# Second block's experts: the two smaller sorted groups share one row tile, 13 units become 11

## The chip, the cores and the metric

The kernel runs on one core of one Trainium2 chip. The metric is the device time of one execution in microseconds (us). The kernel before takes 1627.51 us, the median of 3 runs (1626.91 to 1627.9).

## The reference, cut to what matters

Two blocks run one after the other on 256 tokens of width 1024, in f32. The first is a transformer-like block with 16 experts; the change doesn't touch it. The second has two layers; each is a mixer (attention in three kinds), a norm, and a hierarchical mixture of experts, then a norm again:

```python
lg = jnp.einsum('td,dg->tg', t, rg_w) + rg_b              # 4 groups
g_hot = one_hot(argmax(lg, -1))
le = einsum('tge,tg->te', einsum('td,gde->tge', t, re_w) + re_b, g_hot)   # 8 experts of that group
top_v, top_i = lax.top_k(le, 2)
gate = g_hot * (p_top * gate_e)
for g in range(4):
    h = silu(einsum('td,edf->tef', t, w_gate[g])) * einsum('td,edf->tef', t, w_up[g])
    y = y + einsum('tef,efd->td', h * gate[:, g, :, None], w_down[g])
```

So each token goes to one of 4 groups and there to 2 of 8 experts. An expert has a gate and an up matrix of 1024 x 256 and a down matrix of 256 x 1024: 3 MB in f32. The kernel loads all 32 experts of a layer, 96 MB, whatever the tokens choose.

## The kernel before, in words

**Rows and units.** A layer's experts are done group by group (x = 0 to 3). For a group, its tokens are gathered by a one-hot matrix `PG` into a row tile of at most 128 rows (`group_gather`, two halves); then the rows of each expert are gathered from that tile by a one-hot matrix `PX2` (`expert_gather(u, part)`) into a tile `XS2`, with 64 or 32 columns for each expert. A unit is what one pass of the array takes: 2 experts of 64 rows, or 4 experts of 32 rows. Group 0 has four units of two, in fixed order. Groups 1 to 3 are sorted on the chip by how many tokens an expert has: the four fullest make two units of two, the other four one unit of four. That is 4 + 3 x 3 = 13 units (`UNITS`, line 59).

**One turn of the loop.** In `experts_pe` turn p does, on TensorE: `gate_up(p)` (L1528), the gathers that were put behind it (`slots`, `group_gather`, both L640, `expert_gather`, L1508), `group_sum(p-3)` (L1574), `down(p-2)` (L1557), `turned(p-1)` (L645). At the last unit of a group its one-hot matrix is turned; in the turns of `SHARES` the group's result is spread to the tokens (`group_share`, L1164, from 4 banks). VectorE and ScalarE walk through the same turns in `experts_dve` and `experts_act`. After the last turn come some matmuls that keep the clock up (`keep_on`, L665), the branch of `overflow_pe`, `last_sum()` and the norm.

**The order of the loads.** All weights come in 2 MB blocks through a ring of seven slots, issued by SyncE (`sync`) in the order in which TensorE asks for them: `weights()` appends the key to `order`. A block is issued when TensorE has read the block seven before it. I number a layer's 48 blocks from 0. A unit of two has 2 gate/up blocks and 1 down block; a unit of four has 4 and 2. The turn's order gives gate/up blocks of unit p and then down blocks of unit p-2. Group 0's blocks are single 2 MB transfers (L3195). Blocks of sorted groups (`ranked`, L3154) are put together from 2 transfers of 1 MB or 4 of 512 KB, one for each expert, whose number SyncE reads from SBUF (L3147, 8 numbers at the first block of each group) after VectorE's `by_count` wrote them (`IDS`, L2444).

**The fallback.** Tokens over a capacity (128 rows in a group's tile, 64 or 32 for an expert) set a flag in turn `FLAG_AT`; if it is set, `overflow_pe` and its partners compute the layer's rest again with all 32 experts.

Of the kernel before, what the change touches and what calls it, by code (L numbers as in the profile page):

```python
# [52 lines left out]
CAP = 128  # L53
# [5 lines left out]
UNITS = [(0, j) for j in range(4)] + [(x, j) for x in range(1, 4) for j in range(3)]  # L59
# [4 lines left out]
def four(n):  # L64
    return UNITS[n][0] > 0 and UNITS[n][1] == 2

# [19 lines left out]
def width(u):  # L86

    return 128 if u > 1 and u % 2 else 256


def gathers_behind(n):

    x, j = UNITS[n]
    if x == 0:
        return [(j // 2 + 1, j % 2)]
    if j == 0:
        return [(2 * x + 1, 0), (2 * x + 1, 1)]
    return [(2 * x + 2, 0), (2 * x + 2, 1)] if j == 2 and x < 3 else []

SHARES, FLAG_AT = (8, 11, 13), 10
# [293 lines left out]
def program(nc, ring_d, ranked_d, p1_d, p2_d, pf_d, xT_d, cT_d, pos_d, out_d):  # L396
    order, slot_read = [], []
    with contextlib.ExitStack() as ctx:
# [162 lines left out]
        CAPE, KEY, IDS = take(32), take(4, 8), take(24).bitcast(I32)  # L561
        RK, CMP, PERM, GXP = take(3, 8), take(3, 8, 8), take(3, 8, 8), take(2, 8, 8)
# [563 lines left out]
        def norm_pe(g, l, fresh, turn, full, keep_on):  # L1126

            def last_group(b):
                ps = fresh("ffn", l, 3, b)
                group_share(g, l, 3, b, ps).then_inc(*full("ffn", l, 3, b))  # L1130

            def turned_rows(b):
                ps = PS[:, b, :]
                before, banks.last[b], banks.of["rt", l, b] = banks.last[b], ("rt", l, b), b
                g.wait_ge(*at(*before))
                g.wait_ge(*at("ffn", l, 3, b))
# [30 lines left out]
        def mixers_pe(g, l, fresh, weights, arrived, finished, group, turn, column_sum, across, full, keep_on):  # L1167
# [291 lines left out]
            group(ps[:, 0:32], [(ONES, SEL2[:, ti, 4:36]) for ti in range(2)]).then_inc(*full("cnt", l))  # L1459

        def experts_pe(g, l, weights, arrived, finished, group, turn, full, keep_on):
# [21 lines left out]
            def slots(x):  # L1483

                ps = high("gx", l, x)
                g.wait_ge(*at("posg", l))
                g.wait_ge(*at("gates", l))
                g.wait_ge(*at("pg", l, x > 0))
                group(ps[:, 0:16], [(PG[:, ti, x, :], POSG[:, ti, x, :]) for ti in range(2)]).then_inc(*full("gx", l, x))
# [21 lines left out]
            def gate_up(n):  # L1511
# [3 lines left out]
                for part in range(parts_):  # L1515
# [9 lines left out]
                    for kk in range(nk * part, nk * part + nk):  # L1525
                        for s in range(128 // m):
                            c = (0 if four(n) else (j % 2) * 128) + s * m
                            ins = g.matmul(ps[m * s:m * s + m, :], XS2[u % 2][:, kk, c:c + m], wv[:, kk % nk, s, :], start=kk == 0, stop=kk == 7)  # L1528
# [54 lines left out]
            for p in range(NU + 2):  # L1583
                if p < NU:
                    x, j = UNITS[p]
                    gate_up(p)
                    if j == 0 and x < 3:
                        slots(x + 1)
                    if p == 2:
                        turned_norm()  # L1590
                    if j < 2 and x < 3:
                        group_gather(x + 1, j)
# [29 lines left out]
        def overflow_pe(g, l, group, turn):  # L1622
            g.wait_ge(*at("flag", l))
            with g.If(g.value_load(FLG[0:1, 0:1].bitcast(I32)) > 0):
# [4 lines left out]
                for e in range(32):  # L1629
# [13 lines left out]
                    for m in range(8):  # L1643
                        if m >= 3:
                            g.wait_ge(*at("xrm", l, e, m - 3))
                        group(PS[:, (0, 1, 7)[m % 3], 0:256], [(wd[:, f, m * 128:(m + 1) * 128], XHD[:, f, :]) for f in range(2)]) \
# [451 lines left out]
        def norm_dve(v, l, out, settle, full):  # L2098
# [7 lines left out]
            for b in range(4):  # L2106
                add_share(v, l, 3, b, out, full)
# [37 lines left out]
        def mixers_dve(v, l, out, settle, full, scale_rows, affine, square):  # L2145
# [177 lines left out]
            v.memset(MR, -LOWEST).then_inc(*out())  # L2323
            for b in range(4):
# [85 lines left out]
            v.scalar_tensor_tensor(out=KEY, in0=bank("cnt", l)[:, 0:32].rearrange("p (g e) -> p g e", g=4), scalar=8.0,  # L2410
                                   in1=bc(p1("iotn", 1, 12)[:, :, 0:8], [128, 4, 8]), op0=ALU.mult, op1=ALU.add).then_inc(*out("cnt", l))

        def experts_dve(v, l, out, settle, full):
            sig.stage = f"e{l}"

            def slots(x):
                full("gx", l, x)
                if x == 0:
                    v.tensor_copy(GX[:, x, :], bank("gx", l, x)[:, 0:16]).then_inc(*out("gx", l, x))
                    return  # L2420
                settle()
                v.tensor_tensor(GXP, bc(bank("gx", l, x)[:, 0:16].rearrange("p (a o e) -> p a o e", a=2, o=1), [128, 2, 8, 8]),
                                bc(PERM[:, x - 1:x, :, :], [128, 2, 8, 8]), ALU.mult).then_inc(*out("gx", l, x))
                settle()
                v.tensor_reduce(out=GX[:, x, :], in_=GXP.rearrange("p a r e -> p (a r) e"), op=ALU.add, axis=AX.X, negate=False).then_inc(*out())

            def by_count():

                for x in range(3):
                    v.tensor_tensor(CMP[:, x, :, :], bc(KEY[:, x + 1:x + 2, :], [128, 8, 8]),  # L2430
                                    bc(KEY[:, x + 1, :].rearrange("p (e o) -> p e o", o=1), [128, 8, 8]), ALU.is_ge).then_inc(*out())
# [3 lines left out]
                for x in range(3):  # L2435
                    v.tensor_tensor(PERM[:, x, :, :], bc(RK[:, x:x + 1, :], [128, 8, 8]),
                                    bc(p1("iota")[:, 0:8].rearrange("p (r o) -> p r o", o=1), [128, 8, 8]), ALU.is_equal).then_inc(*out())
                settle()
                for x in range(3):
                    v.tensor_tensor(CMP[:, x, :, :], PERM[:, x, :, :], bc(p1("iotn", 1, 12)[:, :, 0:8], [128, 8, 8]), ALU.mult).then_inc(*out())  # L2440
                settle()
                v.tensor_reduce(out=KEY[:, 1:4, :], in_=CMP, op=ALU.add, axis=AX.X, negate=False).then_inc(*out())
                settle()
                v.tensor_scalar(IDS, KEY[:, 1:4, :].rearrange("p g r -> p (g r)"), -1.0, 8.0, ALU.mult, ALU.add).then_inc(*out("ids", l))  # L2444

            def capacities():

                v.memset(CAPE[:, 0:8], CAPX + 0.5).then_inc(*out())
                v.tensor_scalar(CAPE[:, 8:32], RK.rearrange("p g e -> p (g e)"), 4.5, float(CAPX - CAPQ), ALU.is_lt, ALU.mult).then_inc(*out())
# [3 lines left out]

            def other_groups():
                for ti in range(2):
                    ins = v.tensor_tensor(PG[:, ti, 1:4, :], bc(PSX[:, ti, 1:4].rearrange("p (g o) -> p g o", o=1), [128, 3, 128]),
                                          bc(p1("iota", 1, 128), [128, 3, 128]), ALU.is_equal)
                ins.then_inc(*out("pg", l, 1))
# [17 lines left out]

            def places(x):
                if x >= 2:
                    full("xs2", l, 2 * (x - 2) + 1, 1, 1)
                    full("hd", l, last_unit(x - 2))  # L2480
                settle()
                cols = ((0, 8, 64),) if x == 0 else ((0, 4, 64), (4, 8, 32))
                for e0, e1, m in cols:
                    n, c0 = e1 - e0, 64 * e0
                    px, pxg = [X2[x % 2].rearrange("p e c -> p (e c)")[:, c0:c0 + n * m].rearrange("p (e c) -> p e c", c=m) for X2 in (PX2, PXG)]
                    ins = v.tensor_tensor(px, bc(GX[:, x, e0:e1].rearrange("p (e o) -> p e o", o=1), [128, n, m]),
                                          bc(p1("iota", 1, 128)[:, :, 0:m], [128, n, m]), ALU.is_equal)
                    ins.then_inc(*(out("px", l, x) if e1 == 8 else out()))
                settle()
                for e0, e1, m in cols:  # L2490
                    n, c0 = e1 - e0, 64 * e0
                    px, pxg = [X2[x % 2].rearrange("p e c -> p (e c)")[:, c0:c0 + n * m].rearrange("p (e c) -> p e c", c=m) for X2 in (PX2, PXG)]
                    ins = v.tensor_tensor(pxg, px, bc(GX[:, x, 8 + e0:8 + e1].rearrange("p (e o) -> p e o", o=1), [128, n, m]), ALU.mult)
                    ins.then_inc(*(out("pxg", l, x) if e1 == 8 else out()))
# [30 lines left out]
            places(0)  # L2525
            group_gather(0, 1)
            other_groups()
            expert_gather(0, 0)
            expert_gather(0, 1)
            by_count()  # L2530
            for p in range(NU + 2):
                if p < NU:
                    x, j = UNITS[p]
                    gate_up(p)
                    if j == 0 and x < 3:
# [5 lines left out]
                    if j < 2 and x < 3:  # L2541
                        group_gather(x + 1, j)
                        if j == 1:
                            places(x + 1)
# [11 lines left out]
                if p == FLAG_AT:  # L2556
                    capacities()
                    for ti in range(2):
                        v.tensor_tensor(GOV[:, ti, :, :], PSX[:, ti, 4:36].rearrange("p (g e) -> p g e", g=4),
                                        CAPE.rearrange("p (g e) -> p g e", g=4), ALU.is_gt).then_inc(*out())  # L2560
                        v.tensor_scalar(GOG[:, ti, :], PSX[:, ti, 0:4], float(CAP) + 0.5, None, ALU.is_gt).then_inc(*out())
# [5 lines left out]
                        .then_inc(*out("over", l))  # L2567
                    full("flag", l)
# [9 lines left out]
        def overflow_dve(v, l, settle):  # L2578
            v.wait_ge(*at("flag", l))
            with v.If(v.value_load(FLG[0:1, 0:1].bitcast(I32)) > 0):  # L2580
# [7 lines left out]
                for e in range(32):  # L2588
# [7 lines left out]
                    for m in range(8):  # L2596
                        v.wait_ge(*at("full", "xd", l, e, m))
                        v.tensor_tensor(R[:, m, :], R[:, m, :], PS[:, (0, 1, 7)[m % 3], 0:256], ALU.add).then_inc(*up("dve", "xrm", l, e, m))
# [429 lines left out]
        def experts_act(s, l, out, full):  # L3028
# [56 lines left out]
            for p in range(NU + 2):  # L3085
                if p < NU:
                    x, j = UNITS[p]
                    gate_up(p)
                    if j < 2 and x < 3:
                        group_gather(x + 1, j)  # L3090
# [36 lines left out]
        def sync(q):  # L3127
# [14 lines left out]

            def ranked(i, x, kind, l, group_, j, part):

                if (l, group_) not in experts:
                    q.wait_ge(*at("ids", l))
                    experts[l, group_] = [q.snap(q.value_load(IDS[0:1, 8 * (group_ - 1) + r:8 * (group_ - 1) + r + 1], min_val=0, max_val=7))  # L3147
                                          for r in range(8)]
                of = ranks(j)
                n = SLOT // len(of)  # L3150
                c = n * part + (4096 if kind == "dr" else 0)
                for s, r in enumerate(of):
                    src = ranked_d[3 * l + group_ - 1, bass.ds(experts[l, group_][r], 1), :, c:c + n].rearrange("o p c -> (o p) c")
                    q.dma_start(RING[x][:, s * n:(s + 1) * n], src).then_inc(*land(f"ring{x}", *(("landed", i) if s == len(of) - 1 else ())))  # L3154

            for i, (key, n) in enumerate(order):
# [39 lines left out]
                if key[0] == "dr" and key[2:] == (3, 2, 1):  # L3196
# [288 lines left out]
```

## Time and profile before

| | |
|---|---|
| median of 3 runs | 1627.51 us |
| the profiled execution's own time | 1627.17 us |
| its span, first to last instruction | 1625.4 us |
| TensorE busy in the span | 1407.9 us (87%) |
| 16 DMA queues, share of their time | 74% |
| bytes read from HBM | 490.21 MB |
| mean granted clock | 0.947 |

The execution takes 1.8 us more than its span. Busy shares are averages over stages: the first block's experts, then two times mixer, experts and norm. The second block's experts run from 923 to 1148 us (first layer) and from 1380 to 1603 us (second layer) of the span.

### The profile page before, as it was taken

To read this page: it belongs to the slowest core of one execution; us is meant where nothing else is said; L and a number is where in the kernel's file an instruction comes from. 1 tells how busy PE (TensorE), PEld (TensorE's weight loads), DVE (VectorE), ACT (ScalarE), POOL (GpSimd) and SP (SyncE) were. 2 spreads that over 40 slices of the span, in tenths; PEclk is the share of its full clock that TensorE was granted. 3 is DMA by queue.
4 is the path that set the end of the run, shared out by engine and by line. 5 is a ranking of instruction groups with operands and counts; after the bars stand their busy time and mean duration, and the time that the engine had idled before them with its cause. 6 is when DMAs were issued, how large, how long until landed. Compare 5 with 4: busy or idle time off the path is not lost. (4 is left out here: it accounts for less than half of the span.)

```text
span 1625.4 us, 19345 instructions
## 1 busy us (share of the span) xinstructions
PE 1407.9 (87%) x7684; PEld 789.8 (49%) x7684; DVE 509.0 (31%) x1140; ACT 314.1 (19%) x659; POOL 0.2 (0%) x4
## 2 busy tenths in 40 slices
PE   6999999856656566599999999997999989999978
PEld 4665877412311211166777644432667677444424
DVE  5225553101101101015763522221346744232213
ACT  2422202100000100112332312211223223122202
POOL 0000000000000000000000000000000000000000
PEclk9999999978877878899999999999999999999999
DMA  9465477999999999992321599999715214899993
GB/s 387 167 251 209 165 293 316 412 429 427 427 428 427 428 427 429 427 422 81 145 104 52 216 380 399 411 417 412 315 52 207 98 59 156 345 406 416 418 412 152
DMA packets 56386, 492.62 MB, mean 303 GB/s; under 512 B 6240, under 2 KB 6624, under 8 KB 25952
## 3 DMA queue, kind: packets, MB, share of 16 engines
q1 hardware_dynamic: 56144, 491.15, 74.0%
q8 instruction: 66, 1.08, 0.3%
q14 instruction: 32, 0.26, 0.0%
q10 hardware_dynamic: 144, 0.13, 0.0%
HBM read 490.21 MB, written 1.05 MB: 302 GB/s over the span
## 5 line engine op out<-in xcount | busy, mean ns | idle before, releaser
L640 PE MATMUL PS<-A 128*128 128x256 f32 (+6 forms) x1592 | 376.6, 393 | 5.3 <-ACT A L2624 1.5
L996 PE MATMUL PS<-A 128*32 128x512 f32 x1536 | 237.7, 757 | 135.0 <-DMA A<-ring_d 135.0
L640 PEld LDWEIGHTS PS<-A 128*128 128x128 f32 (+1 forms) x1592 | 277.9, 193 | 96.9 <-issue 57.3
L996 PEld LDWEIGHTS PS<-A 128*32 128x32 f32 x1536 | 52.7, 126 | 306.4 <-issue 238.5
L1528 PE MATMUL PS<-A 128*64 128x512 f32 (+1 forms) x1024 | 188.6, 608 | 12.5 <-DMA A<-ranked_d 12.2
L1528 PEld LDWEIGHTS PS<-A 128*64 128x64 f32 (+1 forms) x1024 | 57.1, 128 | 126.4 <-issue 124.6
L2058 DVE TENSOR_TENSOR A<-A,PS 128x512 f32<-128x512 f32 x8 | 5.5, 687 | 321.0 <-PE PS L996 321.0
L1557 PE MATMUL PS<-A 128*64 128x512 f32 (+1 forms) x512 | 94.9, 597 | 6.7 <-issue 4.7
L645 PE MATMUL PS<-A 128*128 128x128 f32 (+1 forms) x444 | 66.1, 279 | 17.8 <-DVE A L2058 7.1
L645 PEld LDWEIGHTS PS<-A 128*128 128x128 f32 (+1 forms) x444 | 50.0, 143 | 60.4 <-issue 36.0
L2509 DVE TENSOR_TENSOR A<-A,PS 128x256 f32<-128x256 f32 x26 | 11.0, 423 | 194.3 <-ACT A L3059 194.3
L1557 PEld LDWEIGHTS PS<-A 128*64 128x64 f32 (+1 forms) x512 | 27.4, 126 | 70.4 <-issue 66.1
L1391 PE MATMUL PS<-A 128*128 128x256 f32 x256 | 59.3, 383 | 2.3 <-DVE A L2323 1.2
L1391 PEld LDWEIGHTS PS<-A 128*128 128x128 f32 x256 | 47.5, 190 | 11.3 <-issue 3.9
L2515 DVE COPY A<-PS 128x512 f32<-128x512 f32 x26 | 18.0, 692 | 108.3 <-PE PS L1557 108.3
L1574 PE MATMUL PS<-A 128*128 128x512 f32 x104 | 49.5, 597 | 1.8 <-issue 1.8
L3059 ACT ACTIVATE A<-PS 128x256 f32<-128x256 f32 x26 | 10.0, 386 | 204.7 <-PE PS L1528 204.7
L1508 PE MATMUL PS<-A 128*128 128x256 f32 (+1 forms) x256 | 49.3, 343 | 0.0
L1508 PEld LDWEIGHTS PS<-A 128*128 128x128 f32 x256 | 41.0, 190 | 15.0 <-issue 11.4
L665 PE MATMUL PS<-A 128*128 128x256 f32 x156 | 37.5, 389 | 0.0
L2973 ACT ACTIVATE A<-A 128x128 f32<-128x128 f32 (+1 forms) x48 | 21.2, 443 | 73.4 <-DVE A L2285 73.4
L2504 DVE TENSOR_SCALAR A<-PS,A 128x256 f32<-128x256 f32 (+1 forms) x64 | 28.6, 489 | 18.3 <-PE PS L1508 17.6
(360 smaller groups left out, 1302.8 us busy)
## 6 DMA issues: line engine op xcount, KB each, us to landing
A<-ring_d SPq DMA_DIRECT2D x156, 2048.0 KB, 26.6
A<-ranked_d SPq DMA_DIRECT2D x72, 1024.0 KB, 14.2
A<-ranked_d SPq DMA_DIRECT2D x144, 512.0 KB, 15.1
A<-ring_d SPq DMA_DIRECT2D x2, 1312.0 KB, 22.1
A<-ring_d SPq DMA_DIRECT2D x2, 1280.0 KB, 25.2
A<-p_d SPq DMA_DIRECT2D x1, 1232.0 KB, 22.5
A<-xT_d SPq DMA_DIRECT2D x1, 1024.0 KB, 5.5
A<-cT_d SPq DMA_DIRECT2D x1, 1024.0 KB, 12.0
```

Of the source, the lines that this page charges most:

```text
L640: ins = g.matmul(out, l, r, start=n == 0, stop=n == len(pairs) - 1)
L645: return g.transpose(out, in_, ident[0:k, 0:k])
L665: ins = g.matmul(ps[:, 0:256], *(of or (ident, V(o1, 256))), start=True, stop=True)
L996: ins = g.matmul(ps[32 * e:32 * e + 32, :], rows_of(kk, e), wv[:, kk % 2, e, :], start=kk == 0, stop=kk == 7)
L1391: ins = g.matmul(bank("wo", l, b)[:, j * 256:(j + 1) * 256], w[:, k, c:c + 128], O[:, k, :], start=k == 0 and j == 0, stop=k == 7, skip_gr ...
L1508: ins = g.matmul(ps[:, c:c + w], XGT[:, x, d * 128:(d + 1) * 128], px, start=True, stop=True)
L1528: ins = g.matmul(ps[m * s:m * s + m, :], XS2[u % 2][:, kk, c:c + m], wv[:, kk % nk, s, :], start=kk == 0, stop=kk == 7)
L1557: ins = g.matmul(ps[m * s:m * s + m, :], HD[n % 2][:, f, m * s:m * s + m], wd[f][:, s, half * 512:(half + 1) * 512], start=f == 0, stop=f ...
L1574: ins = g.matmul(PS[:, b, :], QT[p % 2], YE2[p % 2][:, half * 512:(half + 1) * 512], start=n == 0, stop=last)
L2504: ins = v.tensor_scalar(XS2[u % 2][:, d, 0:w], bank("xs2", l, u, part, 1)[:, j * 256:j * 256 + w], gain, bias, ALU.mult, ALU.add)
L2515: v.tensor_copy(YE2[p % 2][:, 512:1024], bank("ye2", l, p, 1)).then_inc(*out("ye2", l, p, 1))
L2973: ins = s.activation(p, p, ACT.Exp, bias=ST[:, i, c:c + 1], scale=1.0, accum_out=ST[:, i, 4 + c:5 + c])
```

## The change

`UNITS` becomes 4 + 3 + 4 = 11 units. VectorE finds which of groups 1 to 3 holds the fullest expert (`largest_group`: a one-hot `BIG`). That group is x = 1, and is sorted as before. The other two are joined in one row tile x = 2 (`offsets`, `places_in_groups`): the second group's tokens stand behind the first's. Their 16 experts aren't sorted and are four units of four, 32 rows each. The capacity of 128 rows holds for the joined tile. SyncE reads four expert numbers after the block `("gu", 3, 0)`, four after `("gu", 3, 1)` and two group numbers after `("dn", 4)`, instead of eight at each group's first block. `group_gather` and `slots` of the next tile move to later turns, `FLAG_AT` from 10 to 9, the tests for it to turn 7.

```diff
-UNITS = [(0, j) for j in range(4)] + [(x, j) for x in range(1, 4) for j in range(3)]
+UNITS = [(0, j) for j in range(4)] + [(1, j) for j in range(3)] + [(2, j) for j in range(4)]
 def four(n):
-    return UNITS[n][0] > 0 and UNITS[n][1] == 2
+    return UNITS[n] == (1, 2) or UNITS[n][0] == 2
 def width(u):
-    return 128 if u > 1 and u % 2 else 256
+    return 128 if u == 3 else 256
 def gathers_behind(n):
     x, j = UNITS[n]
     if x == 0:
         return [(j // 2 + 1, j % 2)]
-    if j == 0:
-        return [(2 * x + 1, 0), (2 * x + 1, 1)]
-    return [(2 * x + 2, 0), (2 * x + 2, 1)] if j == 2 and x < 3 else []
-SHARES, FLAG_AT = (8, 11, 13), 10
+    if x == 2:
+        return [(5, j)] if j < 2 else []
+    return {0: [(3, 0), (3, 1)], 2: [(4, 0), (4, 1)]}.get(j, [])
+def halves_behind(n):
+    return {1: (0,), 2: (1,), 4: (0,), 5: (1,)}.get(n, ())
+SLOTS_BEHIND = (1, 4)
+LAST_GROUP = 2
+SHARES, OVER_AT, FLAG_AT = (8, 10), 7, 9
+IDS_BEHIND = {("gu", 3, 0): range(0, 4), ("gu", 3, 1): range(4, 8), ("dn", 4): range(8, 10)}
...
             slots(0)
             places(0)
+            largest_group()
             group_gather(0, 1)
+            offsets()
+            expert_gather(0, 0)
+            places_in_groups()
+            expert_gather(0, 1)
             other_groups()
-            expert_gather(0, 0)
-            expert_gather(0, 1)
             by_count()
+            gated_places(0)
...
+            def read_ids(l, which):
+                q.wait_ge(*at("ids", l))
+                for r in which:
+                    experts[l, r] = q.snap(q.value_load(IDS[0:1, r:r + 1], min_val=0, max_val=47 if r < 8 else 5))
...
-                of = ranks(j)
+                of = ranks(j) if group_ == 1 else range(4 * (j % 2), 4 * (j % 2) + 4)
...
+                if (key[0], *key[2:]) in IDS_BEHIND:
+                    read_ids(key[1], IDS_BEHIND[(key[0], *key[2:])])
```

The new steps on VectorE are small operations on 128 x 1 to 128 x 64 elements: `largest_group` 4, `offsets` 5, `places_in_groups` 6, `other_groups` 8 (4 of 128 x 128) in place of 2 of 128 x 384, `by_count` 13 in place of 12.

## Rows read from the trace of the kernel before

**Rows 1.** Page, part 1: busy time of each engine in the whole span.
```profile
PE 1407.9 (87%) x7684; PEld 789.8 (49%) x7684; DVE 509.0 (31%) x1140; ACT 314.1 (19%) x659; POOL 0.2 (0%) x4
```
**Rows 2.** Windows of the first layer's experts: length, engines busy, clock, DMA share, GB/s.
```profile
950.00:1091.00 141.00, 139.05 (x699) 57.65 (x695) 36.25 (x79) 31.39 (x75) 0.00 (x0) 1.00 1.01 413
1091.00:1144.00 53.00, 43.14 (x221) 17.84 (x221) 9.77 (x19) 5.10 (x13) 0.00 (x0) 0.97 1.03 414
```
**Rows 3.** Timeline of TensorE, second layer's last turns: start us, us, instruction, idle before.
```profile
1573.46 3.21 PE L1528 MATMUL PS<-A 128*32 128x512 f32 x16 [3.19 <-DMA A<-ranked_d]
1578.57 1.92 PE L1528 MATMUL PS<-A 128*32 128x512 f32 x16 [1.90 <-DMA A<-ranked_d]
...
1583.44 3.65 PE L1557 MATMUL PS<-A 128*64 128x512 f32 x16 [1.03 <-DMA A<-ranked_d]
...
1599.27 3.64 PE L1557 MATMUL PS<-A 128*32 128x512 f32 x32 [0.52 <-issue]
```
**Rows 4.** Line 3154 in window 1582:1583, the second layer's last expert transfer.
```profile
L3154 SPq DMA_DIRECT2D A<-ranked_d x1: 1998/1998/1998, 1582.0 to 1582.0; - x1
...
DMA to landing us min/median/max: 17.2/17.2/17.2
```
**Rows 5.** Timeline of TensorE at 691, 1118 and 1144 us.
```profile
691.42 5.34 PE L996 MATMUL PS<-A 128*32 128x512 f32 x32
...
1118.81 3.55 PE L1528 MATMUL PS<-A 128*32 128x512 f32 x16 [3.19 <-DMA A<-ranked_d]
...
1144.04 3.64 PE L1557 MATMUL PS<-A 128*32 128x512 f32 x32
```
**Rows 6.** Chain of waits, second layer's experts: start us, us, what, count.
```profile
1437.15 2.36 PE PS L640 x8
1439.51 1.78 PE PS L1508 x16
1441.29 1.72 PE PS L1574 x4
1443.02 3.58 PE PS L1557 x16
...
1447.08 7.02 PE PS L1528 x32
1454.10 1.92 PE PS L640 x4
...
1461.79 7.00 PE PS L1528 x64
...
1510.10 3.46 PE PS L1164 x16
```
**Rows 7.** Timeline of SyncE at 1446 us: block 19 of the second layer.
```profile
1446.78 2.56 SPq L3154 DMA_DIRECT2D A<-ranked_d  x4
```
**Rows 8.** Its fourth transfer (issued 1449.0), and the first layer's (issued 992.2).
```profile
DMA to landing us min/median/max: 7.4/7.4/7.4
...
DMA to landing us min/median/max: 8.8/8.8/8.8
```
**Rows 9.** DMA in 1523:1543 (1 MB transfers) and 1543:1563 (512 KB transfers).
```profile
DMA packets 1158, 8.42 MB, mean 421 GB/s; under 512 B 130, under 2 KB 130, under 8 KB 130
...
DMA packets 2078, 8.20 MB, mean 410 GB/s; under 512 B 233, under 2 KB 233, under 8 KB 1924
```
**Rows 10.** Expert numbers: written by VectorE, read by SyncE; first transfer behind them.
```profile
926.86 0.18 DVE L2444 TENSOR_SCALAR A<-A 128x24 int32<-128x24 f32 x1
927.17 3.76 SPq L3195 DMA_DIRECT2D A<-ring_d  x2
...
L3147 SPq TENSOR_LOAD <-A x48: 261/264/466, 941.7 to 1513.5; - x48
...
946.51 0.36 SPq L3154 DMA_DIRECT2D A<-ranked_d  x1
```
**Rows 11.** Line 3154 in window 1402.3:1402.6: a 1 MB transfer issued to drained queues.
```profile
DMA to landing us min/median/max: 4.8/4.8/4.8
```

More of the change, by code:

```diff
@@ L1458, in mixers_pe @@
             ps = fresh("cnt", l)
-            group(ps[:, 0:32], [(ONES, SEL2[:, ti, 4:36]) for ti in range(2)]).then_inc(*full("cnt", l))
+            group(ps[:, 0:36], [(ONES, SEL2[:, ti, :]) for ti in range(2)]).then_inc(*full("cnt", l))
         def experts_pe(g, l, weights, arrived, finished, group, turn, full, keep_on):
@@ L1488, in slots @@
                 g.wait_ge(*at("pg", l, x > 0))
-                group(ps[:, 0:16], [(PG[:, ti, x, :], POSG[:, ti, x, :]) for ti in range(2)]).then_inc(*full("gx", l, x))
+                if x:
+                    g.wait_ge(*at("posx", l))
+                n = 32 if x == 2 else 16
+                of = [(POSG[:, ti, 0, :], POSG1[:, ti, :], POSG2[:, ti, :, :].rearrange("p a c -> p (a c)"))[x] for ti in range(2)]
+                group(ps[:, 0:n], [(PG[:, ti, x, :], of[ti]) for ti in range(2)]).then_inc(*full("gx", l, x))
             def turned_norm():
@@ L1590, in experts_pe @@
                         turned_norm()
-                    if j < 2 and x < 3:
-                        group_gather(x + 1, j)
+                    for half in halves_behind(p):
+                        group_gather(x + 1, half)
                     for u, part in gathers_behind(p):
@@ L1645, in overflow_pe @@
                             g.wait_ge(*at("xrm", l, e, m - 3))
[L1646 removed]
+                        group(PS[:, (2, 3, 7)[m % 3], 0:256], [(wd[:, f, m * 128:(m + 1) * 128], XHD[:, f, :]) for f in range(2)]) \
                             .then_inc(*up("pe", "full", "xd", l, e, m))
@@ L2106, in norm_dve @@
             for b in range(4):
-                add_share(v, l, 3, b, out, full)
+                add_share(v, l, LAST_GROUP, b, out, full)
                 if b:
@@ new lines, in other_groups @@
+            def other_groups():
+                settle()
+                for x, where in ((1, AT_BIG), (2, AT_REST)):
+                    for ti in range(2):
+                        ins = v.tensor_scalar(PG[:, ti, x, :], p1("iota"), where[:, ti:ti + 1], None, ALU.is_equal)
+                ins.then_inc(*out("pg", l, 1))
+                v.wait_ge(*at("posg", l))
+                v.tensor_tensor(POSG1, POSG[:, :, 1, :], POSG[:, :, 2, :], ALU.add).then_inc(*out())
+                for a, (g, other) in enumerate(((1, 0), (3, 2))):
+                    v.scalar_tensor_tensor(out=POSG2[:, :, a, :], in0=POSG[:, :, 2, :], scalar=BIG[:, other:other + 1], in1=POSG[:, :, g, :],
+                                           op0=ALU.mult, op1=ALU.add).then_inc(*out())
+                settle()
+                v.tensor_tensor(POSG1, POSG1, POSG[:, :, 3, :], ALU.add).then_inc(*out("posx", l))
@@ L2540, in experts_dve @@
                         normed_rows(p - 3)
[L2541 to L2544, printed above, removed]
+                    for half in halves_behind(p):
+                        group_gather(x + 1, half)
+                    if (x, j) in ((0, 1), (1, 1)):
+                        places(x + 1)
+                        gated_places(x + 1)
                     for u, part in gathers_behind(p):
@@ L3088, in experts_act @@
                     gate_up(p)
-                    if j < 2 and x < 3:
-                        group_gather(x + 1, j)
+                    for half in halves_behind(p):
+                        group_gather(x + 1, half)
                     if 4 <= p < 8:
```

157 lines of the change are left out of this document (105 added, 52 removed).

## The prediction

> **What bounds the kernel now.** I began with the busy times of the page. TensorE is busy for 87% of the span [rows 1], which invites the conclusion that every microsecond of TensorE work removed is one won. That share is a mean over stages, so I read the stage of the change by windows. Through most of the first layer's experts TensorE is full, 139.05 of 141 us, but the DMA share is 1.01 at the same time, with 413 GB/s [rows 2]. Two resources are full together. The windows' second row says which ends last: from 1091 us on TensorE has 9.9 us idle in 53, and the DMA share is still 1.03 [rows 2]. The timeline of the second layer's last turns names the waits: every part of the last `gate_up` waits for its block, 3.19 and 1.90 us, and the parts come 5.11 us apart, though each needs 1.92 us [rows 3]. The last expert transfer is issued at 1582.0 and lands 17.2 us later, at 1599.2 [rows 4]; the last `down` starts at 1599.27 [rows 3]. In the first layer the last `down` starts at 1144.04 [rows 5]. So both layers' experts end when the last of the 48 blocks has landed. What has to be asked of the change is when that block lands, and how fast TensorE does the little that comes behind it.
>
> **TensorE's work: 37 us less in each layer, off the path.** A unit of four costs a turn as much as a unit of two: 64 matmuls in 7.00 us against 32 in 7.02 [rows 6]. Two units go, with 2 x 7.02 (`gate_up`), 2 x 3.58 (`down`), 2 x 1.72 (`group_sum`) and about 2 x 0.5 (`turned`, by the time left between `down` and the next turn). One group goes: two halves of 1.92, its `slots` (2.36 - 1.92 = 0.44), a `group_share` of 3.46; and two narrow gathers of 1.78 [rows 6]. The sum is 14.0 + 7.2 + 3.4 + 1.0 + 3.8 + 0.4 + 3.5 + 3.6 = 36.9 us, 74 in both layers. All of it lies in a stretch in which the DMA queues are full, and the change removes no byte: it is still 48 blocks of 2.097 MB. If TensorE is late nowhere, the sum is 0 from this.
>
> **When the last block lands.** A block is issued only when the one seven before it has been read, so TensorE can still hold the stream back early in the stage. I follow it for the second layer.
>
> Turn 0 loses `slots` and a half gather (-2.36), turn 1 has both where it had one half (+0.44), turn 2 has a half where it had none (+1.92) [rows 6]: 0 for the start of turn 3. Turns 3 and 4 keep their work, with the same 4 gathers of 1.78 or less. So `down(2)` ends as before at 1443.02 + 3.58 = 1446.6 [rows 6]. It frees the slot of block 19, the last gate/up block of the first unit of four, issued at 1446.78 [rows 7]. Before, the queues were still full then, and it landed behind its predecessors, 7.4 us after its fourth transfer, at 1456.4 [rows 8]. After, the stream ahead of it is shorter. SyncE no longer spends 946.5 - 941.7 = 4.8 us reading 8 numbers with a slot free [rows 10], and the blocks behind run 2 to 2.5 us earlier, so that the queues have run dry when block 19 comes. From drained queues a 1 MB transfer lands after 4.8 us [rows 11]; 2.49 of it is data at 421 GB/s [rows 9], the rest, 2.3, is latency. Block 19 then lands at 1446.8 + 2.3 + 5.1 = 1454.2, a gain of 2.2. In the first layer it was issued with the same lead (its fourth transfer at 992.2, landed 8.8 later, at 1001.0 [rows 8]; its first 1.5 before that, at 990.6) and lands at 998.0: a gain of 3.0.
>
> Behind block 19 come 28 blocks. Before they were 14 of two 1 MB transfers and 14 of four 512 KB transfers; now 2 and 26. At 421 GB/s a block takes 4.98 us, at 410 it takes 5.12 [rows 9]. Twelve blocks more of the second kind cost 12 x 0.14 = 1.7 us. From turn 6 on a turn has 6 blocks, 30.7 us of transfers, and at most 7.0 + 3.6 + 1.7 + 3.6 + 0.5 + 3.5 = 19.9 us of TensorE's work, so no slot is late again. Last blocks: 2.2 - 1.7 = 0.5 earlier in the second layer, 3.0 - 1.7 = 1.3 in the first. Together -1.8 us. Between which ends: if the queues never run dry, the 38 blocks from block 10 on take 2 x 4.9 + 6 x 4.98 + 30 x 5.12 = 193.3 us from about 1402.2, when the drained queues of [rows 11] are, and land at 1595.5, 3.7 earlier; 4.6 in the first layer, whose end lies 0.9 later behind its block 19: -8.3. At the other end nothing is won before block 19 and the 1.7 are paid: +3.4.
>
> The Trainium skill speaks against the smaller transfers ("DMA: Bandwidth & Descriptors", section "Bandwidth"): it advises transfers of 1 MiB or more, and its fit has a fixed cost of about 2 us in each. If these costs came one after the other, 24 more transfers a layer would be an estimate of +48 us a layer, by that page alone. The two rates of [rows 9] say that they overlap.
>
> **The short wait for the numbers.** SyncE now reads four numbers behind block 7 (issued at 927.17), and they are written later: 16 small steps more (4 + 5 + 6 + 1) at about 0.18 us [rows 10], some 0.8 more in `other_groups`, less the `PXG` step of 0.7: 926.9 + 0.2 + 2.9 = 930.0. Behind this wait on SyncE stands block 8, which went out at 930.6 (927.17 and 3.76 for the pair, less its own 0.33); with four reads of 0.6 it goes at 932.3 to 932.4, 1.7 late. The gap ahead of block 19 takes that up (it is some 1.5 to 2 us wide). I put 0; the ends are 0 and +1.7 a layer. The next four and two reads lie in waits for slots. On VectorE the new steps lie behind the first `gate_up` (7.0 us), and nothing on TensorE waits for them before turn 1. If that cover failed it would show as a wait in turn 0 or 1, also ahead of block 19.
>
> **The price at the end: a slow clock.** At the last landing before, TensorE had worked without a long break since 1583.44 [rows 3]. Now the last three turns have only `group_sum`, `down` and `turned`, 1.7 + 3.6 + 0.5 = 5.8 us, between landings 10.2 us apart (two blocks each). TensorE idles some 4 us before the last `down`. After an idle time of 3.19 us 16 matmuls took 3.55 us in one place and 3.21 in another, after 1.90 they took 1.92 [rows 3, 5]: the granted clock was at its lower level, 1.2 of 2.4 GHz, and rose within or behind them. Thirty-two matmuls that start so took 5.34 us in the first block [rows 5], against 3.64 at full clock. That is +1.7 a layer, +3.4 together. Nothing hides it: sum, flag branch and norm wait for this `down`. The ends: 0 if the clock stays up, and for a clock that stays low through the `keep_on` behind it, see below.
>
> **Sum.** -1.8 + 3.4 = +1.6, from 1627.17 (profiled execution): 1628.8. The median of the runs stands 0.3 above that execution, so this is 1.3 above the median, and I call it no change: what a measurement of this kernel can tell from none is about 0.2%, 3.3 us.
>
> **Rivals.**
> - *The stream never runs dry, or the clock stays up.* For it: the gap ahead of block 19 is only 1.5 to 2 us wide, and blocks before it landed some tenths late here and there. Against it: the slot of block 19 is freed by TensorE, whose turns 2 to 4 are as long as before. With -8.3 and a clock that stays up it gives 1618.9; with half of it and a clock that stays up, or all of it and a slow start of the last `down`, 1622.3 to 1623.0. Chance 0.22.
> - *The lower clock outlasts the last `down` (slower).* The place is each layer's end. If the clock stays low through all of `down` (3.6 us more) and through the 14 matmuls of `keep_on` (3.3 more, of which some 1.8 goes in the wait for the branch behind), the price is 5.1 a layer; with -1.8 it is 1635.6, and 1632 if only half of it. It decides from a low clock of more than 3.6 us behind the last landing. For it: the stage idles far more than before. Against it: in the first block's rhythm of the same kind it rose within 5.34 us. Chance 0.20. The Trainium skill has this rule ("TensorE: Matmul & The Clock Gate", section "HAM oscillation"): short bursts of matmuls between waits for weights start cold each time. By that rule all turns from 8 on run cold in part; the rows of the first block agree, and there it costs nothing while the next landing is later.
> - *TensorE bounds the stage after all.* 74 us less: 1553. Against it: the DMA share of 1.01 to 1.03. Chance 0.02.
> - *The numbers come much later*, by over 5 us: +3.5 a layer, 1635. Chance 0.02.
> - *It doesn't do what it says:* the fallback runs. It would load 96 MB again, over 240 us a layer at 413 GB/s, so over 1868 for one layer alone. The router of the reference, on its inputs, gives groups of 49, 63, 51, 93 and 62, 96, 43, 55 tokens: 114 and 98 in the joined tile of 128, at most 23 for an expert there. Chance 0.01.
> - *Each small transfer pays its own latency:* 24 x 2.3 = 55 us a layer, 1738, against [rows 9]. The fixed cost in the Trainium skill's fit, above, is of this size. Chance 0.01.
>
> **The numbers.** The forecast (1624.3 to 1630.8, its own range 1625.5 to 1630.8) has 0.52. Faster by over 0.2%: 0.22 + 0.02 = 0.24. Slower: 0.20 + 0.02 + 0.02 = 0.24. The range of 1620 to 1634.5 leaves out the far ends of both sides.
>
> **What would show it.** Right: TensorE's busy time about 60 to 70 us less and its idle time as much more, `L1528` of the last units waiting for DMA 3 us before each part; the DMA share at 1 from block 10 to the end; last landings within 2 us of 1143.9 and 1599.2; last `down` of over 5 us. Wrong: last landings over 3 us earlier (the stream was held back by TensorE more than I read), a wait on TensorE in turns 0 to 2, SyncE waiting for VectorE past 932 us, or a slow clock in the norm.

## The result, and the profile after

The changed kernel takes 1631.0 us (median of 20 runs, 1625.69 to 1634.05), the kernel before 1627.36 us in runs beside them. The ratio is 1.002, 95% interval 1.0012 to 1.0028: slower by about 3.3 us, on the line that the prediction drew between no change and slower. Its profiled execution took 1631.32 us, its span 1629.5 us.

The busy times of the page, which answer to [rows 1]:

```profile
PE 1352.7 (83%) x7532; PEld 756.1 (46%) x7532; DVE 493.5 (30%) x1148; ACT 298.5 (18%) x621; POOL 0.2 (0%) x4
```

TensorE lost 55 us of busy time, and the kernel is slower. The second part of the stage by windows, in both layers, in the columns of [rows 2]; ahead of it, from 950 to 1037 and from 1407 to 1494 us, TensorE is full:

```profile
1037.00:1144.00 107.00, 67.72 (x396) 23.99 (x388) 13.13 (x32) 7.81 (x20) 0.00 (x0) 0.87 1.03 411
...
1494.00:1600.00 106.00, 67.71 (x396) 23.31 (x385) 13.08 (x32) 7.72 (x20) 0.00 (x0) 0.89 1.01 401
```

In this part TensorE now idles 39 of 107 us in the first layer, at a mean granted clock of 0.87, while the DMA share is 1.03; in the second layer it is 38 of 106 us. Most of what was taken from TensorE is there as waiting, the rest as slower matmuls: from the first gate/up matmul to the last `down`, TensorE is busy for 181.7 us in each layer (before: 208.8 and 208.3), though the same work takes 168.7 us at the full clock, as an experiment below shows. The end of the second layer on TensorE, with the first gate/up matmul of the stage ahead of it, answers to [rows 3]; the last transfer, issued at 1584.78, to [rows 4]:

```profile
1379.96 1.51 PE L1543 MATMUL PS<-A 128*64 128x512 f32 x6
...
1568.95 3.54 PE L1543 MATMUL PS<-A 128*32 128x512 f32 x16 [3.20 <-DMA A<-ranked_d]
...
1600.57 6.51 PE L1572 MATMUL PS<-A 128*32 128x512 f32 x32 [4.35 <-issue]
1607.01 3.29 PE L676 MATMUL PS<-A 128*128 128x256 f32 x14
```

```profile
DMA to landing us min/median/max: 15.7/15.7/15.7
```

The last block lands at 1584.8 + 15.7 = 1600.5, 220.5 us behind the first gate/up matmul; in the kernel before it was 219.6 (1599.2 against 1379.6). The last `down` starts at once and takes 6.51 us instead of 3.64 [rows 3], at a granted clock of 0.55. The profile calls the wait ahead of it "issue"; it ends with the landing of the second of its two blocks. The first layer's end, which answers to [rows 5], and SyncE early in that layer, to [rows 10]:

```profile
1144.15 3.64 PE L1572 MATMUL PS<-A 128*32 128x512 f32 x32 [3.09 <-issue]
```

```profile
SPq L3241 <- DVE A L2525: 1.5, 1, 1.5
```

The last `down` starts 221.1 us behind the first gate/up matmul at 923.06 (before: 1144.04 - 923.47 = 220.6) and was quick this time. So the two executions' spans differ by 4.1 us: 0.5 + 1.0 from the landings, 2.9 from the slow `down`, and some tenths of either sign from the mixers, with which the stage's start moves.

### The profile page after: what moved, and what is told of

Read it like the earlier page. It is cut to its first block and busy times, and to the rows that moved or that the text cites. A ratio compares the mean times of both kernels' runs of the same rounds, so it can differ in the third digit from the quotient of the medians.

```text
span 1629.5 us, 18987 instructions
## 1 busy us (share of the span) xinstructions
PE 1352.7 (83%) x7532; PEld 756.1 (46%) x7532; DVE 493.5 (30%) x1148; ACT 298.5 (18%) x621; POOL 0.2 (0%) x4
## 5 line engine op out<-in xcount | busy, mean ns | idle before, releaser
L651 PE MATMUL PS<-A 128*128 128x256 f32 (+5 forms) x1568 | 367.6, 392 | 5.3 <-DMA A<-ring_d 1.6
L1007 PE MATMUL PS<-A 128*32 128x512 f32 x1536 | 233.2, 744 | 139.3 <-DMA A<-ring_d 139.3
L651 PEld LDWEIGHTS PS<-A 128*128 128x128 f32 (+1 forms) x1568 | 274.2, 192 | 90.4 <-issue 51.3
L1543 PE MATMUL PS<-A 128*32 128x512 f32 (+1 forms) x1024 | 168.5, 635 | 40.7 <-DMA A<-ranked_d 40.7
L1572 PE MATMUL PS<-A 128*32 128x512 f32 (+1 forms) x512 | 95.8, 730 | 37.6 <-issue 37.6
L1543 PEld LDWEIGHTS PS<-A 128*32 128x32 f32 (+1 forms) x1024 | 47.1, 124 | 144.6 <-issue 143.6
L656 PEld LDWEIGHTS PS<-A 128*128 128x128 f32 (+1 forms) x428 | 48.3, 143 | 57.5 <-issue 33.1
L1572 PEld LDWEIGHTS PS<-A 128*32 128x32 f32 (+1 forms) x512 | 26.0, 140 | 103.6 <-issue 103.1
L1402 PEld LDWEIGHTS PS<-A 128*128 128x128 f32 x256 | 47.5, 190 | 11.3 <-issue 3.9
L1589 PE MATMUL PS<-A 128*128 128x512 f32 x88 | 41.9, 598 | 2.0 <-issue 2.0
L1523 PE MATMUL PS<-A 128*128 128x256 f32 (+1 forms) x192 | 42.1, 366 | 0.0
L1523 PEld LDWEIGHTS PS<-A 128*128 128x128 f32 x192 | 33.3, 189 | 16.3 <-issue 12.3
L676 PE MATMUL PS<-A 128*128 128x256 f32 x156 | 37.5, 389 | 0.0
L3167 ACT ACTIVATE A<-PS 128x512 f32<-128x512 f32 x22 | 13.1, 598 | 118.4 <-PE PS L1572 118.4
```

Source lines behind the costliest of these rows:

```text
L651: ins = g.matmul(out, l, r, start=n == 0, stop=n == len(pairs) - 1)
L656: return g.transpose(out, in_, ident[0:k, 0:k])
L676: ins = g.matmul(ps[:, 0:256], *(of or (ident, V(o1, 256))), start=True, stop=True)
L1007: ins = g.matmul(ps[32 * e:32 * e + 32, :], rows_of(kk, e), wv[:, kk % 2, e, :], start=kk == 0, stop=kk == 7)
L1402: ins = g.matmul(bank("wo", l, b)[:, j * 256:(j + 1) * 256], w[:, k, c:c + 128], O[:, k, :], start=k == 0 and j == 0, stop=k == 7, skip_gr ...
L1523: ins = g.matmul(ps[:, c:c + w], XGT[:, x, d * 128:(d + 1) * 128], px, start=True, stop=True)
```

## The experiments

Every run is compared with runs of the kernel before on the same chip. I write T for the time from the stage's first gate/up matmul to the landing of the last block; it leaves out how the mixers went. T and the last `down` are read from one profiled execution of each kernel. In the eight layers of the four executions that load as the changed kernel does (the changed one twice, with idle matmuls, filled up) T lies between 220.0 and 221.0, so a difference of 1 us in one pair of layers says little.

| kernel | ratio to before, 95% | T, first and second layer | last `down`, us |
|---|---|---|---|
| before | 1 | 220.4, 219.5 | 3.64, 3.64 |
| changed | 1.002 (1.0012 to 1.0028) | 221.0, 220.5 | 3.64, 6.51 |
| changed, second time | 1.0025 (1.0014 to 1.0036) | 220.1, 220.8 | 3.64, 5.04 |
| changed, idle matmuls ahead of the last `down` | 1.0009 (0.9997 to 1.002) | 220.2, 220.4 | 3.64, 3.64 |
| changed, TensorE filled up | 1.0006 (0.9992 to 1.002) | 220.0, 220.5 | 3.64, 3.64 |
| changed, one transfer a block | 1.0021 (1.001 to 1.0033) | 220.3, 220.2 | 5.29, 5.24 |
| changed, 16 KB rows | 0.9948 (0.993 to 0.9965) | 215.0, 215.5 | 3.64, 5.34 |
| changed, 16 KB rows, idle matmuls | 0.9937 (0.9917 to 0.9958) | 214.4, 215.1 | 3.64, 3.64 |
| the same, 3 idle matmuls behind | 0.9936 (0.9916 to 0.9956) | 214.9, 215.0 | 3.64, 3.64 |
| changed, joined blocks halved | 0.9358 (0.9335 to 0.9381) | 163.5, 163.6 (5.2 and 5.1 us ahead of the last `down`) | 3.64, 3.64 |
| before, 4 KB rows | 1.003 (1.0019 to 1.0042) | 223.7, 222.7 | 3.64, 3.64 |
| before, early expert numbers | 1.0001 (0.9986 to 1.0016) | 219.5, 219.8 | 3.64, 3.64 |
| before, sorted blocks halved | 0.9864 (0.9842 to 0.9887) | 193.4, 193.5 | 3.64, 3.64 |

**The changed kernel once more.** No edit.

> The changed kernel as it is, beside the others of this call. Theory A (the last landing ends each layer's experts, it comes 0.5 to 1 us later against the start of the stage, and TensorE meets it at its lower clock in some executions): +2 to +4 us against the kernel before, last landings 220.5 to 221.5 us behind the stage's first gate/up matmul. Rival B (TensorE's new order of work is what costs, as a wait on VectorE or on a gather): the same time, but block 19 issued later than 67.2 us behind that matmul. Rival C (no difference but the scatter of executions): within 1 us of before.

Measured: 1633.18 against 1629.05 us, +4.1 by the medians, 1.0025 as a ratio. Block 19 is issued 67.14 us behind the first gate/up matmul in both layers, within 0.01 us of the kernel before: TensorE's new order of turns costs nothing up to there (against B), and the difference is there a second time (against C).

**Is TensorE off the path?** Idle matmuls (`keep_on`, 20 each) are put in three turns, where TensorE waits:

```diff
+                if p in (8, 9, 10):
+                    keep_on(20, "fill", l, p, take=high)
                 if p >= 3:
                     group_sum(p - 3)
```

> The changed kernel with 20 idle matmuls of 128x256 (two passes each, 8.9 us) in each of the turns 8, 9 and 10: 27 us of TensorE's work a layer, most of what the change saves. Theory A: it lies in waits for blocks: 0 us, within 1.5 of the changed kernel, last landings as before. Rival B (TensorE is on the path): +27 us a layer, +53.

Measured: 1629.77 us, ratio 1.0006. With 27 us more of TensorE's work in each layer the kernel isn't slower; it is rather faster than the changed one (on the same chip the changed kernel with one transfer a block, below, has 1.0021), and both last `down`s are quick:

```profile
1599.06 3.64 PE L1572 MATMUL PS<-A 128*32 128x512 f32 x32 [1.48 <-issue]
```

**What TensorE alone would need.** Two kernels leave out transfers and no instruction of TensorE. In the changed kernel:

```diff
-                of = ranks(j) if group_ == 1 else range(4 * (j % 2), 4 * (j % 2) + 4)
-                n = SLOT // len(of)
+                of = ranks(j) if group_ == 1 else range(4 * (j % 2), 4 * (j % 2) + 2)
+                n = 1024 if group_ == 2 else SLOT // len(of)
```

> The changed kernel with only the first two of the four experts' 512 KB in each joined block (left out: half of the joined experts' weights; those matmuls run on what lies in the ring). It takes 24 x 2.5 = 61 us of transfers out of each layer and nothing from TensorE. Theory A: the stage gets shorter until TensorE bounds it; its turns need 222 - 37 = about 185 to 190 us where the stream needed 221, so 30 to 36 us a layer, 60 to 72 us less than the changed kernel, and the waits for DMA in the gate/up parts go. Rival B (TensorE's order of work bounds already): under 10 us less.

Measured: 1524.17 us, 104 less than before, far more than I expected. TensorE is full through the window in which it had waits:

```profile
950.00:1091.00 141.00, 141.00 (x833) 56.56 (x831) 35.91 (x77) 28.60 (x69) 0.00 (x0) 1.00 1.00 393
```

The last `down` starts at 1091.00, 168.7 us behind the first gate/up matmul at 922.28. My number was wrong since I took 37 us from the 222 us of the stage before, waits included (it had some 11.6 us of them). The same in the kernel before:

```diff
+                of = of[:len(of) // 2]
                 for s, r in enumerate(of):
```

> The kernel before with only the first half of each sorted block's transfers (left out: half of the sorted experts' weights; those matmuls run on what lies in the ring). 36 x 2.5 = 90 us of transfers less in each layer, nothing less on TensorE. With it the stage's length is TensorE's alone: if the change saves 37 us of TensorE's work a layer, the last down starts 168.3 + 37 = 205 us behind the first gate/up matmul (168.3 was read for the changed kernel with halved blocks), so 15 us a layer, 30 us less than the kernel before. If it stayed near 220, TensorE would have bounded the kernel before.

Measured: 1605.41 us, 22 less than before, where 30 was expected. The last `down` starts 209.95 us behind the first gate/up matmul. In that stand 2.0 us of waiting for VectorE's overflow test and 1.8 in a gate/up of 8.78 us, in part at the lower clock, so TensorE's own work is about 206.2:

```profile
1090.18 0.19 PE L1612 MATMUL PS<-A 128*1 128x1 f32 x2 [1.98 <-DVE A L2566]
1090.49 8.78 PE L1528 MATMUL PS<-A 128*64 128x512 f32 x32
...
1132.79 3.64 PE L1557 MATMUL PS<-A 128*32 128x512 f32 x32
```

206.2 - 168.7 = 37.5 us a layer is what the change takes from TensorE (predicted: 36.9). By this it would bring some 37 us a layer if the weights came in time. With them at 220 us, TensorE's 206 or 169 end nothing.

**Rows or number of transfers?** The part of the change in the transfers, alone in the kernel before:

```diff
+                    if n == 2048:
+                        for h in range(2):
+                            part_ = ranked_d[3 * l + group_ - 1, bass.ds(experts[l, group_][r], 1), :, c + 1024 * h:c + 1024 * h + 1024].rearrange("o p c -> (o p) c")
+                            q.dma_start(RING[x][:, s * n + 1024 * h:s * n + 1024 * h + 1024], part_) \
...
+                        continue
```

> The kernel before, with each 1 MB transfer of the sorted units of two made as two of 512 KB with rows of 4 KB: the part of the change in the transfers alone, in 18 blocks a layer where the change has it in 12. Theory A: 18 x 0.14 = 2.5 us a layer, +5 us. Rival B (TensorE bounds the stage, as its 87% suggest): 0. Rival C (a fixed cost of about 2 us for each transfer): 36 more transfers a layer, +72 us a layer.

Measured: 1633.08 us, ratio 1.003, +4.9 us. T grows by 3.3 and 3.2 us, somewhat more than 2.5. This part alone, in 18 blocks a layer where the change has it in 12, makes the kernel before as slow as the changed one.

Then the changed kernel with one transfer for each joined block, rows of 4 KB as they were:

```diff
+                if group_ == 2:
+                    src = ranked_d[bass.ds(experts[l, 8 + j // 2], 1), of[0]:of[0] + 4, :, c:c + n].rearrange("o e p c -> p (o e) c")
+                    q.dma_start(RING[x].rearrange("p (e c) -> p e c", e=4), src).then_inc(*land(f"ring{x}", "landed", i))
+                    return
```

> The changed kernel with each of the 24 blocks of joined experts as one transfer of 2 MB, but rows of 4 KB as before: 72 transfers a layer fewer, the same rows. Theory A1 (the length of the rows sets the 5.12 us of a block): the time of the changed kernel, within 1.5 us; 144 to 145 us from block 19's landing to the last. Theory A2 (the number of transfers sets it): the time of the kernel with 16 KB rows, 11 us less; 139 us.

And with rows of 16 KB, from a second copy of the joined weights (`joined`), laid out by halves of a group:

```diff
+                if group_ == 2:
+                    src = joined_d[bass.ds(experts[l, 8 + j // 2], 1), j % 2, part + (4 if kind == "dr" else 0), :, :].rearrange("o p c -> (o p) c")
+                    q.dma_start(RING[x], src).then_inc(*land(f"ring{x}", "landed", i))
+                    return
...
+    joined = np.ascontiguousarray(ranked.reshape(6, 2, 4, 128, 6, 1024).transpose(0, 1, 4, 3, 2, 5)).reshape(6, 2, 6, 128, 4096)
```

> The changed kernel with the weights of the 16 joined experts laid out in the device's memory a second time, four experts side by side, so that each of the 24 blocks of joined experts is one 2 MB transfer with rows of 16 KB, not four of 512 KB with rows of 4 KB. Theory A (the stage is a stream of 48 blocks): a block of 16 KB rows takes 4.89 us (429 GB/s, as in the first block's experts) and not 5.12, so 24 x 0.23 = 5.5 us a layer, 11 us less than the changed kernel and 7 to 9 less than before. Rival B (TensorE or SyncE sets the end): 0. Rival C (each small transfer pays a fixed cost that doesn't overlap): much more than 11 us.

Measured: 1631.88 us (1.0021) for the one transfer, 1620.26 us (0.9948) for the rows. The DMA of the window 1540:1560 in four kernels: changed, one transfer, and 16 KB rows; then 4 KB rows in the kernel before, in 1530:1550.

```profile
DMA packets 2241, 8.19 MB, mean 409 GB/s; under 512 B 246, under 2 KB 246, under 8 KB 2239
...
A<-ranked_d SPq DMA_DIRECT2D x17, 512.0 KB, 15.0
```

```profile
DMA packets 2055, 8.18 MB, mean 409 GB/s; under 512 B 62, under 2 KB 62, under 8 KB 2053
...
A<-ranked_d SPq DMA_DIRECT2D x5, 2048.0 KB, 24.5
```

```profile
DMA packets 585, 8.53 MB, mean 426 GB/s; under 512 B 64, under 2 KB 64, under 8 KB 64
```

```profile
DMA packets 2243, 8.18 MB, mean 409 GB/s; under 512 B 248, under 2 KB 248, under 8 KB 2242
```

17 issues or 5, the rate is 409 GB/s as long as the rows have 4 KB; with 16 KB it is 426. So A2 and the fixed cost of a transfer fall. Between rows of 8 and of 4 KB the length is shown to set the rate: the kernel before with 4 KB rows reads the same array, with the same 24 KB from row to row, at 409 instead of 421 GB/s. With 16 KB rows each block is also one contiguous stretch of the device's memory, and no run tells the long row from the contiguous block. T is 6.0 and 5.0 us shorter than in the changed kernel's first execution (predicted 5.5 a layer).

**Is it the clock at the end?** `keep_on` issues idle matmuls of 128x256 whose result nobody reads; here 7 of them (the profile counts each twice, x14) ahead of the last `down`:

```diff
+                if p == NU + 1:
+                    keep_on(7, "wait", l, take=high)
                 if 0 <= p - 2 < NU:
                     down(p - 2)
```

> The changed kernel with 7 idle matmuls of 128x256 on TensorE in the last turn, between group_sum and the last down, where it waits 3.1 and 4.4 us for the last block. Theory A: the last down takes 3.6 us in both layers, not up to 6.5; 1.5 to 3 us less than the changed kernel, so within 2 us of before. Rival B (a low clock isn't the cause, TensorE's queue is only made longer): 0 to +1 us, the last down as long as without.

Measured: 1629.06 us, ratio 1.0009 beside 1.0025 for the changed kernel on the same chip: 2.6 us less by the ratios (4.1 by the medians, 2.5 by the means of the 12 runs; the two intervals overlap). The filled kernel, whose last `down`s are quick too, is 2.4 us below the one with one transfer a block by the ratios, both measured on another chip than this pair. The two comparisons agree; neither is far outside the scatter by itself. The last `down`, in the second layer:

```profile
1595.98 3.18 PE L676 MATMUL PS<-A 128*128 128x256 f32 x14
1600.09 3.64 PE L1572 MATMUL PS<-A 128*32 128x512 f32 x32 [0.93 <-issue]
```

and without the matmuls ahead of it, in the second execution of the changed kernel:

```profile
1599.78 5.04 PE L1572 MATMUL PS<-A 128*32 128x512 f32 x32 [3.88 <-issue]
```

In the first layer of that execution the last `down` was quick, and the clock fell behind it: the four matmuls of `last_sum` (L1589) took 3.65 us at a granted clock of 0.53, where they take 1.96 in the first execution:

```profile
1151.98 3.65 PE L1589 MATMUL PS<-A 128*128 128x512 f32 x4 [2.18 <-issue]
```

**Both.**

> Both: the joined experts' blocks with rows of 16 KB, and the 7 idle matmuls ahead of the last down. Theory A: the two add, as one moves the last landing and the other what TensorE does behind it: 8 to 9 us less than before from the first, 2 to 3 from the second where the last down began slow, so 10 to 12 us less than before; last downs of 3.64 us. Rival B (the slow clock lies elsewhere as much): no better than the rows alone, -8.5.

Measured: 1617.89 us against 1628.18, ratio 0.9937: 10.3 us less than before, as the two together should bring; against the 16 KB rows alone (0.9948) the 1.8 us of the idle matmuls aren't clear of noise. They also cost something: in both layers the last `down` starts 0.5 us behind the last landing, where it is 0.1 without them, since they ran past it. Then 3 idle matmuls behind the last `down` in place of 7 (`keep_on(3, "flag", ...)`):

> The kernel with 16 KB rows and the idle matmuls ahead of the last down, with 3 idle matmuls behind it in place of 7. Behind the last landing everything is on the path. If the 7 are longer than what the branch and the copies behind the last down need, 0 to 1.8 us a layer less, up to 3.6 us less than with 7, 13 to 14 less than before. If they cover it, 0; if the clock falls without them, slower by up to 4.

Measured: 1617.84 us, ratio 0.9936. In the profile the way from the last `down`'s end to the end of the kernel went from 22.46 to 20.88 us, but the times don't show it. In the first layer `last_sum` took 3.28 us instead of 1.96, at a granted clock of 0.57, which takes back most of that. Either is faster than both kernels of the case.

**One more part of the change, alone in the kernel before:**

```diff
+                if (key[0], *key[2:]) in (("gu", 3, 0), ("gu", 3, 1)):
+                    l_, half = key[1], key[3]
...
+                    experts[l_, 1] += [q.snap(q.value_load(IDS[0:1, r:r + 1], min_val=0, max_val=7)) for r in range(4 * half, 4 * half + 4)]
```

> The kernel before with one part of the change alone: the first sorted group's eight numbers are read behind blocks 7 and 8, not at block 10. Theory A: block 10 goes out 4.8 us earlier, block 19's issue stays at +67.1 us (TensorE sets it) and its landing moves from +77.1 to about +75.9, so the last landings come 1.2 us earlier in each layer, 2.4 us less than before. Rival B (the queues run dry ahead of block 19 and take all of it): 4 us less. Rival C: 0.

Measured: ratio 1.0001. Block 19's landing moved from 77.5 and 76.7 to 76.2 and 76.4 us behind the first gate/up matmul, 1.2 us as expected in the first layer and 0.4 in the second, and T is 219.5 and 219.8 against 220.4 and 219.5. No gain can be told. The interval excludes B's 4 us less; the 2.4 of A lie just outside it too (its lower end is -2.3).

## Why the prediction was right, and where it was off

**What bounds the stage: right.** The 37 us of TensorE's work a layer are gone (37.5 by the two halved kernels) and brought nothing; putting 27 back cost nothing. TensorE's idle time in the stage went from 11.6 to 39 us a layer. Its busy time fell by 55 us and not by the 60 to 70 named as a sign: in each layer the matmuls that started at the lower clock took back some 13 us of it (181.7 busy where the work takes 168.7 at the full clock), against some 2 before. Ahead of the last `down` that cost nothing, as it lay in waits.

**When the last block lands: wrong in sign, one term mis-sized.** I had -1.8 us for both layers; the first execution shows +0.6 and +1.0, the second -0.3 and +1.2. TensorE's part of it was right: block 19's issue stays at 67.14 us. The stream ahead of it was right too: block 17 lands 2.4 us earlier than before in both layers. And the queues did run low when block 19 came. In the 3 us behind its issue they moved 283 GB/s in the second layer, where the kernel before moved 404 in the same place:

```profile
1447.00:1450.00 3.00, 3.00 (x17) 1.11 (x18) 0.69 (x1) 0.55 (x2) 0.00 (x0) 1.00 0.90 283
```

```profile
1446.70:1449.70 3.00, 3.00 (x17) 1.11 (x18) 0.69 (x1) 0.55 (x2) 0.00 (x0) 1.00 1.02 404
```

The DMA share of 0.90 hardly shows this; the GB/s do. The failed step is the price of it, "lands at 1446.8 + 2.3 + 5.1 = 1454.2": 7.4 us from block 19's issue to its landing. It took 8.4 us in the second layer and 8.8 in the first. Block 18's fourth transfer, issued at 1439.2, landed 11.1 us later, at 1450.3, 3.2 us behind the issue of block 19 at 1447.1, so the queues were low and not empty. Block 19's fourth, issued at 1448.7, landed 6.9 us later, at 1455.5:

```profile
DMA to landing us min/median/max: 11.1/11.1/11.1
```

```profile
DMA to landing us min/median/max: 6.9/6.9/6.9
```

Of the 2.4 us won at block 17, 1.3 were left at block 18 and 1.2 at block 19 in the second layer, 1.8 and 1.5 in the first. I had put 2.2 and 3.0 at block 19. That is 2.5 us too much for both layers; why blocks 18 and 19 each took longer than the 5.1 us of a full stream is open.

Behind block 19 I put +1.7 us for twelve more blocks with 4 KB rows; 28 blocks took 145.0 us in both layers, before 143.0 and 142.8, so +2.1, and +1.3 and +1.8 in the second execution. In the eight layers of the four executions that load alike it is 144.5 on the mean, 1.6 to 1.7 more than before, so this term was right. Their mean T is 220.4, against 220.0 before: +0.9 for both layers, where one profiled execution of the kernel before is all there is to compare with. The kernel before with 4 KB rows agrees in kind. That the rows are the cause, and not the count of transfers, the prediction only argued; now it is shown. The 48 us a layer that it worked out for costs one after the other rest on a figure for other transfers: the Trainium skill has the fixed cost of about 2 us ("DMA: Bandwidth & Descriptors", section "Anatomy of one DMA — SWDGE (gpsimd) path") for transfers issued from GpSimd. Here SyncE issues them, and 72 transfers a layer fewer at the same rows changed nothing.

**The wait for the numbers: right.** SyncE waited 1.5 us for VectorE, and block 8 went out at 931.0, 8.0 us behind the first gate/up matmul where it had been 7.1: 0.8 us late in this layer, 0.6 in the other, and not 1.7. The price was put at 0, and block 9 went out earlier than before.

**The slow clock at the end: right as a mechanism, in size on the mean only.** I had 5.34 us for each of the two last `down`s. Four executions of it without cover, two of the changed kernel and one each of the kernels with one transfer and 16 KB rows, have eight of them (the table): 3.64 three times, and 5.04, 5.24, 5.29, 5.34 and 6.51. The mean is 4.79, 1.15 more than 3.64, +2.3 for both layers where I had +3.4. The three quick ones stand behind the shorter idle times, 2.35, 2.60 and 3.09 us, the five slow ones behind 2.87 to 4.35; one pair is out of order. Behind one of the quick ones the clock fell later, in `last_sum`: that comes close to the sign "a slow clock in the norm", and cost 1.7 us in one of the eight layers. The idle matmuls took the slow `down`s away and brought 2.6 us, about the size of the term.

**The sum.** Predicted -1.8 + 3.4 = +1.6; by the runs +0.9 (mean T of four executions) to +1.2 (of the two of the changed kernel itself), and +2.3 for the last `down`s or +2.7 with the slow `last_sum`, together 3.2 to 3.9, beside a measured 3.3 to 4.1. The likeliest time was 1628.8, the measured 1631.0: inside the range of 1620 to 1634.5, but 0.2 us above the narrower one of 1625.5 to 1630.8 that had the chance of 0.52. The effect of 0.2% (0.12 to 0.28) excludes zero. That the total came so close is in part luck: the stream was put 2.7 to 3.0 us too low and the clock 0.7 to 1.1 us too high, and the two errors have opposite signs. The rival of a clock that stays low through the `keep_on` behind the last `down` didn't come about: `keep_on` took its 3.29 us each time.

## What to carry to other kernels

When two resources are full in the same window, work taken from the one that doesn't end last turns into waiting; look for the last landing, and price the change in what it does to the bytes and their rows. A joined or regrouped load is an occasion to lay its weights out in long rows, one block in one contiguous piece: that was worth 12 us here, when the regrouping itself was worth nothing. Behind a stage that waits for transfers, the first work after the last landing met a slow clock in five of eight layers here; a few idle matmuls ahead of it took that away. Keep them shorter than the wait: in the three kernels with 7 of them the last `down` started 0.4 to 0.9 us behind the landing in five of six layers, where it is otherwise 0.1.

## What the runs showed of the hardware

- For loads queued on SyncE the rate depends on the row: 409 GB/s at 4 KB, 421 at 8 KB [rows 9], 426 at 16 KB with contiguous blocks; 5 transfers or 17 in 20 us made no difference.
- Where the queues ran low it showed in the GB/s more than in the DMA share: 283 against 404 GB/s, at a share of 0.90 against 1.02.
- The same 32 matmuls took 3.64 us behind idle times of 2.35, 2.60 and 3.09 us, and from 5.04 to 6.51 us behind idle times of 2.87 to 4.35 us. In the second execution's slow one the granted clock was 0.72, in its quick one 1.00.
- Repeated executions of one kernel spread over 6.6 us (before) and 8.4 us (changed), more than the difference in question. The times from one event of the stage to another (67.14 or 67.15 us to block 19's issue, in all twelve kernels) were far steadier, and T stayed within 1.0 us in the eight layers that load alike; so they tell parts apart where the times can't, down to about 1 us.
